# Between the two scans of a DeltaNet and RWKV block: one branch's output projection and 12 gate tiles placed among the pieces of the second scan

## The reference, cut to what matters

```
a_lat, b_lat, gates_lat = jnp.split(u_lat @ w_in, split_at, axis=-1)
oa_lat, _ = run_a(a_lat, state_a)                       # branch A: gated delta rule
ob_lat, _ = run_b(to_col_major(b_lat, rows), state_b)   # branch B: RWKV-7
g_a, g_b = jnp.split(gates, 2, axis=-1)
y = jax.nn.sigmoid(g_a) * (o_a @ w_o_a) + jax.nn.sigmoid(g_b) * (o_b @ w_o_b)
return y @ w_out
```

```
w_log = -softplus(-(w0 + tanh(w_lo) @ w2)) - 0.5 ;  iclr = sigmoid(a0 + a_lo @ a2)
sa = einsum('vk,k->v', s, a_t)
s  = s * w_t + sa b_t^T + v_t k_t^T ;  y_t = s r_t
```

## Time and profile before

| | |
|---|---|
| time, median of 3 | 2577.27 us |
| time of the profiled execution | 2579.31 us |
| its span in the trace | 2577.6 us |
| PE busy in the span | 2447.0 us (95%) |
| DVE / ACT / POOL busy | 1410.0 / 1197.7 / 302.8 us |
| shift stage, about | 1750 to 1865 us |
| scan, about | 1867 to 2127 us |
| merge up to `out2`, about | 2127 to 2220 us |

### The profile page before, as it was taken

The page is one execution under the profiler, slowest core; times in us unless marked ns, Lnnn a source line. Parts: engine busy times, 40 slices in busy tenths (PEclk is TensorE's granted clock), DMA queues, the critical chain, the costliest instruction groups (busy, mean ns, idle before and its releaser), DMA issues.

```text
span 2577.6 us, 52450 instructions
## 1 busy us (share of the span) xinstructions
PE 2447.0 (95%) x23247; PEld 2117.1 (82%) x23247; DVE 1410.0 (55%) x2198; ACT 1197.7 (46%) x1733; POOL 302.8 (12%) x425
## 2 busy tenths in 40 slices
PE   6999999999999999999999999999988879999998
PEld 5999887799999998878899985686467768868877
DVE  4654545366646645442666555464445542178886
ACT  4434456434344434474444345431254432177775
POOL 0100000031101100000301000461133322000000
PEclk8999999999999999999999998999989999999999
DMA  6764522356656754322557512101200003379995
GB/s 216 241 208 156 185 98 99 115 191 202 221 188 201 243 176 168 133 99 98 177 177 235 206 47 93 68 4 38 94 7 4 4 4 103 131 236 367 366 362 187
DMA packets 269172, 396.08 MB, mean 154 GB/s; under 512 B 9352, under 2 KB 172861, under 8 KB 268813
## 3 DMA queue, kind: packets, MB, share of 16 engines
q1 hardware_dynamic: 267209, 389.25, 44.2%
q0 software_dynamic: 1120, 2.17, 0.3%
q10 hardware_dynamic: 612, 1.24, 0.1%
HBM read 391.59 MB, written 1.05 MB: 152 GB/s over the span
## 4 chain that ended last, share of the span: by engine, by line
PE 76%; DVE 7%; issue 6%; DMA 5%; ACT 4%; POOL 2%; SPq 0%; ACTq 0%; POOLq 0%; DVEq 0%
PE ps L282 75%; DMA RB<-in_moe_w_up 4%; DVE gwl L431 2%; POOL H L1415 1%; ACT gwh L422 1%; POOL AR L2541 0%; ACT wh L422 0%; PE ps L1093 0%; ACT AR L2758 0%; DVE wl L431 0%; ACT AR L2750 0%; DMA RB<-in_ffn_w_gu 0%; DVE AT L1178 0%; DVE AR L1677 0%; DVE AR L1901 0%
## 5 line engine op out<-in xcount | busy, mean ns | idle before, releaser
L431 DVE TENSOR_TENSOR wl<-RB,wh 128x2048 fp32r<-128x2048 f32 (+4 forms) x188 | 413.5, 2201 | 294.8 <-ACT wh L422 294.2
L282 PE MATMUL ps<-H,RB 128*128 128x256 f32 (+1 forms) x1712 | 453.9, 422 | 1.1 <-ACT H L1515 1.1
L422 ACT ACTIVATE wh<-RB 128x2048 fp32r<-128x2048 f32 (+4 forms) x188 | 342.1, 1823 | 237.0 <-PE ps L282 205.4
L282 PEld LDWEIGHTS ps<-H,RB 128*128 128x128 f32 x1712 | 324.8, 193 | 114.1 <-issue 76.8
L282 PE MATMUL ps<-xhf,wl 128*128 128x256 f32 x1408 | 404.4, 287 | 13.9 <-DVE xlf L651 9.2
L282 PE MATMUL ps<-xlf,wh 128*128 128x256 f32 x1408 | 401.1, 285 | 0.0
L282 PE MATMUL ps<-xhf,wh 128*128 128x256 f32 x1408 | 401.0, 285 | 0.0
L282 PE MATMUL ps<-AR 64*64 64x64 f32 (+3 forms) x8296 | 263.6, 236 | 47.3 <-issue 18.4
L282 PEld LDWEIGHTS ps<-AR 64*64 64x64 f32 (+2 forms) x8296 | 231.5, 142 | 78.4 <-issue 50.0
L282 PEld LDWEIGHTS ps<-xhf,wl 128*128 128x128 f32 x1408 | 273.1, 194 | 24.9 <-DVE wl L431 14.7
L282 PEld LDWEIGHTS ps<-xlf,wh 128*128 128x128 f32 x1408 | 273.1, 194 | 0.1
(11 more groups left out here) (441 smaller groups left out, 4158.4 us busy)
## 6 DMA issues: line engine op xcount, KB each, us to landing
RB<-in_ffn_w_gu SPq DMA_DIRECT2D x88, 1024.0 KB, 7.7
RB<-in_w_in SPq DMA_DIRECT2D x25, 2048.0 KB, 7.8
RB<-in_ffn_w_down SPq DMA_DIRECT2D x16, 2048.0 KB, 7.8
RB<-in_w_gate SPq DMA_DIRECT2D x16, 2048.0 KB, 8.9
RB<-in_moe_w_gate SPq DMA_DIRECT2D x32, 1024.0 KB, 7.7
RB<-in_moe_w_up SPq DMA_DIRECT2D x32, 1024.0 KB, 10.2
RB<-in_moe_w_down SPq DMA_DIRECT2D x32, 1024.0 KB, 8.3
RB<-in_ada_w SPq DMA_DIRECT2D x12, 2048.0 KB, 9.9
```

Of the source, the lines that this page charges most:

```text
L282: return M.matmul(o, lhsT, rhs, start=start, stop=stop, skip_group_check=True)
L422: S.activation(self.pair(h)[0], of(slot_of(*key)), ACT.Copy).then_inc(*did("high", *mark))
L431: V.tensor_tensor(lo, of(slot_of(*key)), hi.bitcast(F32), ALU.subtract).then_inc(*did("low", *mark))
```

## The change

- **Pieces of the merge enter the scan's order.** New pieces `merge0` (a tile of o_a @ w_o_a), `gate0` (a tile of the first gate half, in two steps) and `gate1` (a tile of the second half) stand in `rwkv_order`. Of `merge0` and `gate0` all eight tiles of each are there, of `gate1` tiles 0 to 3: 32 + 64 + 32 = 128 products of 256 columns. In unit 0's preparation: merge0 0, gate0 0, merge0 1. Slot -1: gate0 1, merge0 2, gate0 2. Slots 0, 1 and 2: one merge0 in the middle and one gate0 at the end. Slot 3: merge0 6 and gate0 6 ahead of `mid` 2, merge0 7 in the middle, gate0 7 at the end. Slots 4 and 5: a gate1 at the end. Slot 7: gate1 2 and gate1 3. The merge keeps gate1 4 to 7.
- **GpSimd's products** (`weigh`) stand behind its product of `prep` 3 and, for tile 7, in slot 4. They write Y0. For branch B the gate is applied by VectorE straight from PSUM (`yb_v`), in place of ScalarE's copy and GpSimd's product.
- **Bank use.** merge0 and gate0 use bank 4 (the first three pieces banks 3 and 4), gate1 in the scan uses banks 5 to 7.
- **`base_b` now stands ahead of the next `prep` 0** on every engine.
- **No meetings.** Both `everyone` calls are gone; each engine waits for what it reads. The copies of W2, A2, W0 and G2 move into the shift stage's last steps, and the last sigmoid of the shift stage (GLO) behind `prep` 1 of unit 0. GpSimd's sixteen row DMAs of the merge wait for unit 7's `kt` and `bon_in` instead of the meeting.
- **The ring** loads the gate tiles 8 to 15 ahead of o_b.

```diff
-            order = prepared(0, *range(7)) + [(("products", 0, o),) for o in range(2)]
+            order = prepared(0, 0, 1) + fill(("merge0", 0, 0)) + prepared(0, 2) + fill(*gate(0), ("merge0", 1, 0))
+            order += prepared(0, *range(3, 7)) + [(("products", 0, o),) for o in range(2)] + fill(("weigh", 0, 0))
+            sigmoid = {-1: gate(1), 3: [("merge0", 6, 0)] + gate(6)}
+            weigh = {-1: [("weigh", 1, 0)], 3: [("weigh", 5, 0), ("weigh", 6, 0)]}
+            weigh.update({i: [("weigh", i + 2, 0)] for i in (0, 1, 2)})
+            middle = {i: [("merge0", i + 3, 0)] for i in range(-1, 3)}
+            middle[3] = [("merge0", 7, 0)]
+            end = {i: gate(i + 3) for i in range(-1, 3)}
+            end[3] = gate(7)
+            end.update({4: [("gate1", 0, 0)], 5: [("gate1", 1, 0)]})
...
-                slot = [solve(n, "base_a", 0)] + prepared(p, 0) + [solve(n, "base_b", 0)]
+                slot = [solve(n, "base_a", 0), solve(n, "base_b", 0)] + prepared(p, 0)
...
-                slot += prepared(p, 1)
+                slot += prepared(p, 1) + fill(*sigmoid.get(i, ())) + (fill(("weigh", 7, 0)) if i == 4 else [])
...
-                slot += [unit(i, "early", 1) + out(i, "out", 0)] + prepared(p, 3)
+                slot += [unit(i, "early", 1) + out(i, "out", 0)] + prepared(p, 3) + fill(*weigh.get(i, ()))
+                slot += fill(("gate1", 2, 0)) if i == 7 else fill(*middle.get(i, ()))
...
+                slot += fill(("gate1", 3, 0)) if i == 7 else []
...
-                slot += [unit(p, "products", 0), unit(p, "products", 1), solve(n, "more", 5)]
+                slot += [unit(p, "products", 0), unit(p, "products", 1), solve(n, "more", 5)] + fill(*end.get(i, ()))
...
-            everyone(("moved", 14), ("low_act", 14), ("rv_rows", 3), ("unit_kk", 3))
...
+                if what == "merge0":
+                    sv = slot_of("o", 0).rearrange("p (k n) -> p k n", k=4)
+                    PE.wait_ge(*landed("o", 0))
+                    PE.wait_ge(*at("o_rows", 1))
+                    ps = bank(("merge", 0, i), ("yb", 0, i), among=kept if i > 1 else (3, 4))
+                    for k in range(4):
+                        ins = mm(ps[:, 0:T], sv[:, k, 128 * i:128 * i + 128], OAT[:, k, :], k == 0, k == 3)
+                    ins.then_inc(*did("merge", 0, i))
+                elif what == "gate0":
+                    sv = slot_of("mgate", 0, i // 4).rearrange("p (k n) -> p k n", k=KD)
+                    if x == 0:
+                        PE.wait_ge(*landed("mgate", 0, i // 4))
+                        bank(("mgate", 0, i), ("mgated", 0, i), among=kept if i else (3, 4))
+                    ps = ps_of("mgate", 0, i)
+                    for k in range(4 * x, 4 * x + 4):
+                        ins = mm(ps[:, 0:T], sv[:, k, 128 * (i % 4):128 * (i % 4) + 128], HA[:, k, :], k == 0, k == KD - 1)
...
+            def gate1_act(c):
+                AC.wait_ge(*at("mgate", 1, c))
+                S.activation(SG1[c], ps_of("mgate", 1, c)[:, 0:T], ACT.Sigmoid).then_inc(*did("mgated", 1, c))
...
-            everyone(("ya", 7, 1), ("ya", 6, 1), ("bon", 7), ("uu", 7, 1))
...
-                branch_pe(0, OAT)
+                for c in range(4, KD):
+                    gate1_pe(c, every_bank)
...
-                    DV.wait_ge(*at("weighed_b", 1, c))
-                    V.tensor_tensor(YB[0][:, c, :], YB[0][:, c, :], YB[1][:, c, :], ALU.add).then_inc(*did("summed", c))
+                    DV.wait_ge(*at("merge", 1, c))
+                    DV.wait_ge(*at("mgated", 1, c))
+                    V.tensor_tensor(SG1[c], ps_of("merge", 1, c)[:, 0:T], SG1[c], ALU.mult).then_inc(*did("yb_v", c))
+                    DV.wait_ge(*at("yb_v", c))
+                    V.tensor_tensor(Y0[c], Y0[c], SG1[c], ALU.add).then_inc(*did("summed", c))
```

More of the change, by code:

```diff
@@ L2364, in unit, with fill, gate @@
                 return [(what, i, x)] if 0 <= i < 8 else []
-            order = prepared(0, *range(7)) + [(("products", 0, o),) for o in range(2)]
+            def fill(*pieces):
+                return [(piece,) for piece in pieces]
+            def gate(c):
+                return [("gate0", c, 0), ("gate0", c, 1)]
+            order = prepared(0, 0, 1) + fill(("merge0", 0, 0)) + prepared(0, 2) + fill(*gate(0), ("merge0", 1, 0))
[8 more added lines that the diff above has]
+            end.update({4: [("gate1", 0, 0)], 5: [("gate1", 1, 0)]})
             for i in range(-1, 8):
@@ L2737, in scan_act @@
                     u = units[i]
-                    if what == "prep" and x == 0:
+                    if what == "merge0":
+                        AC.wait_ge(*at("merge", 0, i))
+                        if i > 1:
+                            AC.wait_ge(*at("weighed_b", 0, i - 2))
+                        S.activation(YBR[i % 2], ps_of("merge", 0, i)[:, 0:T], ACT.Copy).then_inc(*did("yb", 0, i))
+                    elif what == "gate0" and x:
+                        AC.wait_ge(*at("mgate", 0, i))
+                        if i > 1:
+                            AC.wait_ge(*at("weighed_b", 0, i - 2))
+                        S.activation(SGB[i % 2], ps_of("mgate", 0, i)[:, 0:T], ACT.Sigmoid).then_inc(*did("mgated", 0, i))
+                    elif what == "gate1":
+                        gate1_act(i)
+                    elif what == "prep" and x == 0:
+                        AC.wait_ge(*at("moved", 13))
                         if i:
@@ L2971, in tensor @@
                 PE.wait_ge(*at("ob", 1))
-                branch_pe(1, OBT)
+                sv = slot_of("o", 1).rearrange("p (k n) -> p k n", k=4)
+                PE.wait_ge(*landed("o", 1))
+                for c in range(KD):
+                    ps = bank(("merge", 1, c), ("yb_v", c))
+                    for k in range(4):
+                        ins = mm(ps[:, 0:T], sv[:, k, 128 * c:128 * c + 128], OBT[:, k, :], k == 0, k == 3)
+                    ins.then_inc(*did("merge", 1, c))
                 for c in range(KD):
```

137 lines of the change are left out of this document (73 added, 64 removed).

## The result

The changed kernel takes 2555.46 us (median of 4, 2553.87 to 2557.19) against 2577.97 of the kernel before on the same chip: ratio 0.9912, 95% interval 0.9895 to 0.9929. The predicted 2542 is 13 us too low; the time lies in the range of 2533 to 2558, but outside the forecast's own 2536 to 2549. The profiled execution took 2556.89, which is 22.4 less than that of before. I had summed up 35.3.

A forecast was written before the change was run, and what follows sets the result against it. PE was taken to pace the merge, PE and a four-engine chain in turn the scan. 12.5 + 6.9 + 9.7 + 4.0 + 2.2 = 35.3 us off 2579.31 gave 2544.0, less 2.0 to the median: 2542, range 2533 to 2558.

The forecast's parts named there:

- Part 1: Scan's start: without the meeting PE goes straight on at full clock, pieces cover idle time; 12.5 us gained.
- Part 2: Slot -1: work at half clock runs at full clock, pieces cover two waits, base waits open; 6.9 us gained, at worst 0.
- Part 3: Slots 0 to 6: pieces cover waits for base_b, base, exponentials and bonus, less slot 3's bank wait; 9.7 us gained.
- The clock as a whole: Half-clock time expected to go: 4.9 us at the scan's start, 6.3 in slot -1, 1.0 in the merge.
- Part 4: Scan: four of PE's 18 instruction-fetch stops vanish near pieces; 4 us gained, leaving 12 to 16 of 18.3.
- Part 5: Slot 7 and merge: 0.7 us of waits covered, 1.5 from clock and second meeting; 2.2 gained, merge about 36 us.
- A: Rival: the clock falls at the scan's start all the same; gain 24.1 us, 2553; chance 0.13.
- B: Rival: pieces cover nothing in the scan, each wait stands behind the piece again; gain 19.5 us, 2558; chance 0.14.
- C: Rival, slower: all 17 pieces on bank 4 wait 1.7 us each for its release; 2587; chance 0.03.
- D: Rival, better: fetch stops vanish wherever PE's line lengthens and the bank wait is covered; gain 45 us, 2532; chance 0.08.

The follow-up runs named there:

- meeting: Changed kernel with all engines meeting ahead of the scan again and the low-rank weights copied behind the meeting: 2565.41 us, ratio 0.9955.
- lump: Changed kernel with ring loads held back and the pieces of slots -1 to 3 in one row between slots 1 and 2: 2579.57 us.
- lump_banks: As lump, but the row's pieces take banks 5 to 7 in turn in place of bank 4: 2573.78 us, ratio 0.9983.
- changed_again: Second measurement of the unaltered changed kernel, on one chip beside paced_again: 2557.47 us, ratio 0.9932.
- no_loads: Changed kernel with the three 2 MB weight loads in the scan cut to 32 KB each, so it multiplies old weights: 2548.84 us, ratio 0.9892.
- paced: Changed kernel with gate tiles 8 to 11 loaded earlier in eight 256 KB DMAs, the other two loads held to the scan's end: 2547.05 us.
- paced_again: Second measurement of paced, on one chip beside changed_again: 2550.32 us, ratio 0.9891.
- paced2: As paced, with gate tile 6 moved to slot 3's middle, o_a tile 7 one place on, gate tiles 10 and 11 one place ahead: 2547.92 us.

## Why the prediction was right in direction and 13 us short

**Part 1, meeting and clock: right.** 12.5 us expected; the stretch from the last shift tile to unit 0's products is 5.5 us shorter with 6.9 us of pieces in it: 12.4. The products start 5.5 us sooner behind the last shift tile (5.6 expected), the stop left ahead of them is 1.5 us, as put. Undoing it (meeting) brought back stop and half clock.

**Part 2, slot -1: right.** Clock 1.00 all through it in this execution (in lump, which has no pieces in this slot, it was not); the open base waits are 1.6 us (1.4 expected).

**Part 3, slots 0 to 6: right, a little low.** The bank wait in slot 3 is 1.31 us (1.7 expected). All waits but issue fell by 23.4 us; my terms for them (4.3, 3.3, 2.0 - 1.4, 9.7, 0.7, 0.5) are 19.1. lump and lump_banks have 17.7 and 10.8 us of half clock where the changed kernel has 6.0 and 8.7. The pieces may thus keep the half clock away as well, for which I had put down nothing in the scan behind slot -1, but the spread between profiles leaves that unproven.

**The clock as a whole: right in size.** 17.4 us were lost to it before and 6.0 after, 11.4 less (8.7 less by changed_again); my terms are 4.9 + 6.3 + 1.0 = 12.2. The spells that I expected to go, at the scan's start and in the merge, are gone; about 4 of the 6.0 us are new and stand beside and behind the two long stops.

**Part 4, "issue": this step failed.** I put -4.0 with 12 to 16 us left; measured is +8.5, and +2.4 by the second profile of the same kernel. What I had left out are the loads. I had read from the earlier trace rows that blocks of instructions travel over the DMA engines at one in 4.3 us, and from the earlier trace rows that PE uses them up in about 4, and I had looked at the ring's loads only for whether the weights arrive in time ("the ring has every tile tens of us early"). That they come in the middle of the scan, at 366 and 388 GB/s in two windows of 5 us, with the DMA engines full, was in the diff and in my own remark on the ring; I never put the two together. Without them, in no_loads, the sum of the table is 35.5, which is 9.6 and 7.9 us less than in the two profiles of the changed kernel: part in the stops, part in the half clock behind them. The smaller part: the 4 us for stops that pieces let vanish did not come either. With the pieces in their places, the four executions without a long stop (no_loads, paced, paced_again, paced2) have 16.7 to 22.3 us of "issue", against 18.3 before. A likely reason is that PE, where other waits went, reached the end of a block sooner and waited there instead, so that a covered wait is partly given back as a stop; but the difference is smaller than the spread, and no run shows it. The Trainium skill ("Runtime: NRT & Kernel Launch", section "Instruction fetch mechanics") calls these refills mostly hidden; in no execution here did they cost PE less than 16.7 us.

**Part 5, merge: right in size.** 36.4 us (36 expected), VectorE's chain hidden, PE waits there only for the gated output and its turned copies, 0.8 and 1.1 us, as before (0.9 and 1.1). New is a stop of 0.56 us just ahead of `out2`, which no block of instructions explains.

The measured 2555.5 lies between the times of rivals A (2553) and B (2558), so the time alone could not have told them from my forecast; the trace does. A falls by the clock of 1.00 at the scan's start, B by the waits that went from 35.7 to 12.3, C by its one bank wait, D by "issue", which did not fall. C was also counted wrongly: the kernel puts 14 of the tiles on bank 4, and not 17, and at 1.7 us for each of the 14 C would have been about 2582 and not 2587.

By the profile first shown, the error of 12.9 us (35.3 less 22.4) is -12.5 in part 4, +4.3 in the other waits, -0.8 in the clock, and some 4 which no column holds. By changed_again it is 12.3: -6.4, +2.6, -3.5 and some 5. Both say the same in sum: 7 to 9 us were lost inside the columns, and 4 to 5 outside, 1.1 of them behind `out2` in the first. In no_loads the sum fell by 35.9 against the 35.3 of the forecast, though not term by term. So the loads account for the first part, and the second stays open.

## What to carry to other kernels

When work is moved, list the DMAs that its finished buffers release, and look at what the engines read over the DMA engines at that time, the instructions of TensorE among it. In a stretch of dense small products cut a prefetch into pieces behind marks of the program, or hold it until large tiles run. Independent tiles are worth most one by one ahead of the waits of a chain: in a row they left 27 to 31 us of other waits, in their places 12 to 16. And judge a step of a few us by the rows of the place in question, since the whole time moved by more than that between executions of one kernel.

## What the runs showed of the hardware

- Every stop of PE that waits for nothing in the profile, some 270 between 1862 and 2160 us in fourteen traces, ended 2.2 to 3.0 us after the start of a block of instructions on a DMA queue.
- Loads of 2 MB, 283 to 326 GB/s in the mean over the load or the pair, delay these blocks in dense stretches: 6.3 to 8.9 us from one to the next, with stops of 2.7 to 3.8 us in six kernels. At the same places without a load (no_loads, paced, paced_again) it is 3.7 to 5.1 us, and stops of at most 1.6.
- A load of the same size beside slow products made no stop (PE busy for 7.40 of 7.40 us).
- Stops of 2.7 us and more for such a block, eleven in seven traces, each went with a half clock of 3 to 10 us, and so did the stops of 3.9 to 4.4 us behind a meeting; one of 2.8 us for VectorE in lump did not. The half clock also came and went without such a stop, in executions of one and the same kernel too (6.0 and 8.7 us lost in the two profiles of the changed kernel; 9.5 in paced2, with no stop above 2.1 us). Whether that makes the spread between runs of one kernel (11 us in changed_again) stays open.
